# Two transformer-style blocks on one core: where the quarters of a modulation product stand inside the mixer's weight tiles

## The reference, cut to what matters

```python
def modulation(cvec, w, b):
    m = jax.nn.silu(cvec) @ w + b
    return jnp.split(m[..., None, :], 6, axis=-1)
...
sh1, sc1, g1, sh2, sc2, g2 = modulation(c, w_mod[i], b_mod[i])
csh1, csc1, cg1, csh2, csc2, cg2 = modulation(c_ctx, w_mod[i], b_mod[i])
h = x * (1.0 + sc1) + sh1
hc = xc * (1.0 + csc1) + csh1
...
qa, ka, va, ga, qb, kb, vb, gb, lr = split_cols(h @ w_in, EVEN_SPLITS)
...
x = sublayer_residual(x, y, g1, ln_g[i, 0], ln_b[i, 0])
```

## Time and profile before

| | us |
|---|---|
| runs, median (lowest to highest) | 1282.27 (1280.57 to 1283.77) |
| the profiled execution, its own time | 1283.15 |
| its span in the profile | 1281.3 |
| PE (matmuls) busy in the span | 1239.1 (97%) |
| PE weight loads busy | 1151.2 (90%) |
| DVE busy | 888.1 (69%) |
| ACT busy | 572.2 (45%) |
| POOL busy | 97.5 (8%) |

### The profile page before, as it was taken

How to read it: one execution, slowest core, us unless ns; L and a number is a source line. 1 busy time by engine, 2 the same in 40 slices (tenths; PEclk the granted TensorE clock), 3 DMA queues, 4 the chain that set the end, 5 groups by cost and what they waited for, 6 DMA issues and landing times.

```text
span 1281.3 us, 23866 instructions
## 1 busy us (share of the span) xinstructions
PE 1239.1 (97%) x10185; PEld 1151.2 (90%) x10185; DVE 888.1 (69%) x1381; ACT 572.2 (45%) x894; POOL 97.5 (8%) x144
## 2 busy tenths in 40 slices
PE   6999999999999999999999999999999888999997
PEld 3899999999988788999998998998999768999997
DVE  4667765677574665587686786786888966767656
ACT  4433347644775454545313213213165655534441
POOL 0111112100001111000010011120100000000000
PEclk8999999999999999999999999999999999999999
DMA  9997898656245463232554456675435103455550
GB/s 345 384 311 240 264 251 204 165 164 195 72 165 174 156 198 132 100 99 87 176 150 137 150 175 197 188 238 161 135 118 198 34 2 132 165 182 182 195 165 34
DMA packets 170283, 218.44 MB, mean 170 GB/s; under 512 B 6224, under 2 KB 147993, under 8 KB 170042
## 3 DMA queue, kind: packets, MB, share of 16 engines
q1 hardware_dynamic: 140328, 148.18, 35.5%
q0 software_dynamic: 29152, 67.42, 17.4%
q10 hardware_dynamic: 698, 1.32, 0.3%
HBM read 215.77 MB, written 1.12 MB: 169 GB/s over the span
## 4 chain that ended last, share of the span: by engine, by line
PE 87%; ACT 4%; DMA 3%; DVE 3%; issue 1%; SPq 1%; POOL 0%; DVEq 0%; ACTq 0%
PE bank L1388 32%; PE bank L723 13%; PE bank L742 10%; PE bank L775 7%; PE bank L758 4%; DMA graw_b<-in_w_mod 2%; PE bank L1293 2%; PE bank L1366 2%; PE bank L833 1%; PE bank L1483 1%; PE bank L1466 1%; PE bank L1545 1%; PE bank L924 1%; DMA pre<-in_w_ada 1%; PE bank L1000 1%
## 5 line engine op out<-in xcount | busy, mean ns | idle before, releaser
L2207 DVE TENSOR_TENSOR wlo<-raw,whi 128x2048 fp32r<-128x2048 f32 x131 | 297.4, 2275 | 88.3 <-ACT whi L1588 87.9
L1588 ACT ACTIVATE whi<-raw 128x2048 fp32r<-128x2048 f32 x131 | 247.9, 1899 | 182.7 <-PE bank L1388 130.4
L1388 PE MATMUL bank<-a_lo,whi 128*128 128x256 f32 (+1 forms) x688 | 165.3, 312 | 0.0
L1388 PE MATMUL bank<-whi,m_hi 128*128 128x256 f32 x576 | 161.0, 279 | 1.2 <-DVE m_lo L2854 0.8
L1388 PE MATMUL bank<-whi,m_lo 128*128 128x256 f32 x576 | 160.3, 278 | 0.0
L1388 PE MATMUL bank<-wlo,m_hi 128*128 128x256 f32 x576 | 160.3, 278 | 0.0
L1388 PEld LDWEIGHTS bank<-a_lo,whi 128*128 128x128 f32 x688 | 112.1, 188 | 8.8
L1388 PEld LDWEIGHTS bank<-whi,m_hi 128*128 128x128 f32 x576 | 108.9, 189 | 1.9 <-DVE m_lo L2854 1.2
L1388 PEld LDWEIGHTS bank<-whi,m_lo 128*128 128x128 f32 x576 | 108.8, 189 | 0.0
L1388 PEld LDWEIGHTS bank<-wlo,m_hi 128*128 128x128 f32 x576 | 108.4, 188 | 0.1
L723 PE MATMUL bank<-h_hi,whi 128*128 128x256 f32 x368 | 104.2, 283 | 0.0
(11 more groups left out here) (459 smaller groups left out, 3200.1 us busy)
## 6 DMA issues: line engine op xcount, KB each, us to landing
raw<-in_mlp_w SPq DMA_DIRECT2D x64, 1024.0 KB, 5.2
raw<-in_w_in SPq DMA_DIRECT2D x32, 1024.0 KB, 7.4
graw_b<-in_w_mod POOLq DMA_DIRECT2D x64, 512.0 KB, 5.1
raw<-in_ev_w_in SPq DMA_DIRECT2D x12, 1024.0 KB, 5.2
pre<-in_w_ada SPq DMA_DIRECT2D x16, 512.0 KB, 9.8
graw_a<-in_w_mod POOLq DMA_DIRECT2D x16, 512.0 KB, 6.7
Y<-in_w_mod POOLq DMA_DIRECT2D x16, 512.0 KB, 4.1
raw<-in_od_w_qkv SPq DMA_DIRECT2D x6, 1024.0 KB, 4.9
```

The costliest lines, as they stand in the source:

```text
L1388: mm = nc.tensor.matmul(o, x, y, start=(k == 0 and i == 0), stop=(k == KT - 1 and i == 2))
L1588: nc.scalar.activation(split_pair(u, kt * cols)[0], landing(u, kt * cols), ACT.Copy).then_inc(hi_done, 1)
L2207: nc.vector.tensor_tensor(split_pair(u, n)[1], landing(u, n), bf(whi[u % HI], n), ALU.subtract).then_inc(lo_done, 1)
```

## The change

`mix_tile` issues the two quarters of a row tile one by one, one behind each half tile. Before, both stood behind the second half. Units E+7 and E+8 keep two quarters behind each tile. The same 32 quarters are computed, in the same order.

```diff
                 if u in (MIX_QT, MIX_KT):
                     col_unit(u, a_hi, a_lo, T, before[u], (i, i + 1))
-                else:
-                    row_unit(u, a_hi, a_lo, (2 * i, 2 * i + 1), before[u] + i, part)
-                if u < U_EV + 12 and 1 in part:
-                    quarters(2)
+                    if u < U_EV + 12:
+                        quarters(2)
+                    return
+                for n in part:
+                    row_unit(u, a_hi, a_lo, (2 * i, 2 * i + 1), before[u] + i, (n,))
+                    if u < U_EV + 12:
+                        quarters(1)
```

## The result

The changed kernel takes 1292.93 us (median of 4 runs, 1290.32 to 1294.39), the kernel before 1281.91 us (4 runs, 1280.57 to 1283.77). The ratio is 1.0084, with a 95% interval from 1.0066 to 1.0102: 11 us slower. The forecast was 1292.5 us.

A forecast was written before the change was run, and what follows sets the result against it. PE, busy for 97% of the span, was taken to bound the kernel; 3.5 (breaks, E+4) + 5.9 (`mod_done`) - 2.2 (loads) + 3.0 (clock) = +10.2 us on 1282.27 gave 1292.5 us, range 1287.5 to 1296.

The forecast's parts named there:

- The wait for `mod_done`: First quarters come half a tile earlier and wait for DVE's take_mod in E+5, E+6 and E+9: +5.9 us net.
- The clock: PE's clock falls to half for 3.4 us behind each of the two long waits, E+5 and E+9: +3.0 us.
- The rival that it stays up: PE's clock stays up behind one or both long waits: 1291.0 or 1289.5 us, chance 0.27.
- The breaks: Quarters in the middle of ten row tiles make PE leave the tile, 0.33 us each: 3.3 us.
- Unit E+4: Two moved quarters beside decay_sums cost 0.2 us each, 0.4 us; the first fills a 0.2 us wait for ACT.
- The loads: Quarters' loads start one by one instead of in pairs, so PE's three waits for a load go: -2.2 us.
- the loads still collide: Rival: lone loads issued near a unit's 1 MB load need 7.5 us, several tiles wait; 1294 to 1296 us, chance 0.10.
- The sum: All terms for the mixer together: +10.2 us, added to the median of 1282.27 us, gives 1292.5 us.
- Nothing gave it back: Behind 510 us PE's one short wait for DVE hangs on PE's own head_sums(7), so no added time is recovered.

The follow-up runs named there:

- e1: The changed kernel with take_mod(10), take_mod(11) and take_mod(14) moved ahead in DVE's queue; ratio 1.0021 to the kernel before, 1284.14 against 1281.15 us.
- e8: The changed kernel with take_mod(10) alone moved ahead in DVE's queue; ratio 1.006 to the kernel before.
- e3: The changed kernel with only the first tiles of E+5, E+6, E+9, E+10 and E+11 split; ratio 1.0119 to the kernel before, 1296.94 us.
- e4: The changed kernel with the first quarter behind three quarters of the first tiles of E+5, E+6 and E+9; 1286.12 us, ratio 1.0041 to the kernel before.

## Why the prediction was right, point by point

- **The wait for `mod_done`.** Forecast 3.06, 0.3 and 3.31 us; the rows show 3.19, 0.38 and 3.30, and no wait in E+10 and E+11. e1 and e8 show it is the cause: where DVE is earlier, it's gone.
- **The clock.** Forecast a fall behind both waits, 3.4 us at half clock, 1.5 us each. It fell behind both, 3.4 us each, and cost 1.4 us each (1.00 us in the half tile, 0.43 in the quarter). The rival that it stays up falls. The evidence for it was thinner than the prediction says: its three falls lay behind waits of 2.2 to 2.7 us in one trace, and other executions show waits of 2.27 to 2.39 us without a fall. Behind waits as long as these two (2.64 us and more) it fell every time, so the forecast wasn't luck.
- **The breaks.** Forecast 0.33 us each. In the five second tiles, which wait for nothing in either kernel, the mean from the first matmul to the next step is 6.69 us before and 7.07 us after, leaving out a gap of 0.2 us in two of them: 0.38 us a break (0.2 to 0.5 in the five). Taken for all ten that is 3.8 us instead of 3.3. The term was a little small. Those two gaps, 0.4 us in all (ahead of L1196, "issue"), are there in every run that splits E+9's and E+11's second tiles, and no row says what they wait for: that stays open.
- **Unit E+4.** Forecast 0.4 less 0.2 us. From its first matmul to `head_turn(0)` it takes 17.97 us after and 18.11 before, 0.1 us less. The filled wait was worth more than the two quarters beside `decay_sums` cost. So the rule of the Trainium skill, "TensorEngine Tiling (Array Packing)", key properties, that I weighed there (a full price at `decay_sums` as well) doesn't show at that place, while the 0.38 us of a break in a tile agrees with it. No run shows that a drain is what those 0.38 us are.
- **The loads.** Forecast -2.2 us, and PE has no wait for a load left. The three late pairs of the kernel before took 0.66, 0.68 and 0.88 us more from quarter to quarter than the 0.43 of a pair without a wait, 2.2 us. The page gives 4.3 us as the median landing of a quarter, against 5.1 before:

```profile
graw_b<-in_w_mod POOLq DMA_DIRECT2D x64, 512.0 KB, 4.3
```

In the working of this term two things were wrong without harm to the sum. The first is the reason for the slow pair. The pair of the earlier trace rows was issued 0.9 us behind a 1 MB load of a unit (484.6 us). The pair of the kernel before at 458.3 us, with no unit's load beside it, and the lone load of the changed kernel at 474.1 us, 0.8 us behind a unit's, took:

```profile
DMA to landing us min/median/max: 4.1/4.4/4.6
...
DMA to landing us min/median/max: 6.1/6.1/6.1
```

So what made the pair land late was the unit's load in flight with it more than its being a pair, and splitting the pair doesn't end that: in the changed kernel the five lone loads issued within 1.3 us behind a unit's took 5.7 to 6.3 us, the others 3.9 to 4.3. The rival "the loads still collide" had that right and its price wrong: they took 6.3 us at most, the quarters they were for came at least 7.3 us behind the issue, and none was late. The second is that I said that the space between first quarters is larger than a landing everywhere, and didn't look at E+9, whose loads start behind an unsplit pair. There a wait of 1.3 us was ready (e1), under the wait for `mod_done`.
- **The sum.** Measured parts: 3.8 + 0.4 - 0.1 for breaks, gaps and E+4, 6.9 less 0.8 for `mod_done`, -2.2 for loads, +2.9 for the clock: 10.9 us, and the mixer grew by 10.8. Forecast 10.2. Between the medians of the runs it is 11.0 us. That the time of 1292.5 us is met within 0.4 us is in part luck: the growth was forecast 0.8 us too small, and the median that it was added to, 1282.27 us, lies 0.4 us above the one of all four runs.
- **Nothing gave it back.** Behind E+12 both kernels have the same single wait of 0.6 us for DVE, and PE's queue carried the growth to the end.

## What to carry to other kernels

When work with a wait is moved ahead in an engine's queue, first look up when what it waits for is ready: here the load was the visible wait, and the semaphore of a slower engine, 0.2 and 0.5 us late before, was 3 us late half a tile earlier. Everything behind the waiting instruction moves with it. To fill a short wait of PE, move the waiting work back behind a step that is there anyway, rather than cut a run of matmuls for it: that gave 3.4 us where the cut cost 10.8, and where even with `mod_done` there in time the cut cost 2.4 (e1).

## What the runs showed of the hardware that I had not expected

- A wait of PE can have two prices. Each of the seven idle times of 2.64 to 3.30 us in the mixer (changed kernel, e3, e8), whether for DVE or for a load, was followed by 3.4 us at half clock and cost 1.4 to 1.6 us more. Idle times of 1.79 and 1.89 us (e4) cost only themselves, but idle times between 1.83 and 2.39 us elsewhere went either way, at the same place in the program, from one profile to the next.
- Two waits at one instruction hide each other. The load in E+9 that was late by 1.31 us in e1 doesn't show in the changed kernel at all, though by its landing it would have held the quarter up by 1.4 us.
- A load of 512 KB took 3.9 to 4.3 us alone in the changed kernel and 5.7 to 6.3 us close behind a unit's load of 1 MB.
- A quarter of eight matmuls costs PE 0.43 us behind another one, and 0.81 us (0.43 and the 0.38 of a break) where it stands by itself in a tile.
